# Attention entries on un-normalised input, and rotary partners fetched by DMA: a fused fp32 block on one core

## The reference: what is computed

```python
def apply_rope(x, cos, sin):            # DA and DSA; SWA rotates part of the head only
    x1, x2 = jnp.split(x.astype(jnp.float32), 2, axis=-1)
    return jnp.concatenate([x1 * c - x2 * s, x2 * c + x1 * s], axis=-1)
# SWA: softmax over a band with a sink, output times silu(gate)
h = h + diff_attention(rms_norm(h, da_norm), da_w_qkv, ...)   # a = p1 - lam * p2, 8 heads
h = h + dsa_attention(rms_norm(h, dsa_norm), dsa_w_in, ...)   # 16 heads, masked by the index
```

## Time and profile before

| | us |
|---|---|
| median of three runs | 2396.76 |
| lowest, highest | 2393.91, 2399.07 |
| profiled execution, its own time | 2399.34 |
| its span | 2397.2 |
| mean granted TensorE clock of it | 0.941 of full speed |

### The profile page before, as it was taken

The page is one execution under the profiler, slowest core; times in us unless marked ns, Lnnn a source line. Parts: engine busy times, 40 slices in busy tenths (PEclk is TensorE's granted clock), DMA queues, the critical chain, the costliest instruction groups (busy, mean ns, idle before and its releaser), DMA issues. The chain is left out here.

```text
span 2397.2 us, 41216 instructions
## 1 busy us (share of the span) xinstructions
PE 2217.2 (92%) x15151; PEld 1943.4 (81%) x15151; DVE 1466.3 (61%) x3053; ACT 1014.1 (42%) x1857; POOL 47.8 (2%) x37
## 2 busy tenths in 40 slices
PE   5999996979996799997999999989899889999998
PEld 3777775857774688885999999977777679999997
DVE  6778786354554566765566663359667656666522
ACT  4555554234443345554444342233455444443322
POOL 1000000000000000000000000021200000000000
PEclk7999996989997899997999999988999879999998
DMA  4533412343210211111233333311111123333330
GB/s 121 142 101 102 108 53 57 92 75 79 55 35 20 69 54 47 49 44 36 85 91 87 87 107 90 85 53 36 50 36 44 35 62 88 87 87 94 104 92 35
DMA packets 361349, 172.36 MB, mean 72 GB/s; under 512 B 67647, under 2 KB 359336, under 8 KB 361256
## 3 DMA queue, kind: packets, MB, share of 16 engines
q1 hardware_dynamic: 360616, 170.28, 26.0%
q0 software_dynamic: 640, 0.87, 0.3%
HBM read 168.68 MB, written 2.16 MB: 71 GB/s over the span
## 5 line engine op out<-in xcount | busy, mean ns | idle before, releaser
L277 PE MATMUL ps<-h_parts,parts 128*128 128x264 f32 (+1 forms) x8672 | 1337.7, 313 | 28.8 <-DVE h_parts L301 16.4
L277 PEld LDWEIGHTS ps<-h_parts,parts 128*128 128x128 f32 x8672 | 1196.8, 190 | 128.7 <-issue 32.6
L236 ACT ACTIVATE parts<-ring 128x1024 fp32r<-128x1024 f32 (+1 forms) x286 | 311.1, 1092 | 736.4 <-PE ps L277 501.6
L252 DVE TENSOR_TENSOR parts<-ring,parts 128x1024 fp32r<-128x1024 f32 (+1 forms) x270 | 341.4, 1268 | 248.1 <-ACT parts L236 247.1
L277 PE MATMUL ps<-wide_parts,parts 128*128 128x264 f32 (+1 forms) x1152 | 351.0, 305 | 0.0
L277 PE MATMUL ps<-up_hidden,parts 128*128 128x264 f32 x1408 | 257.8, 285 | 1.7 <-PEq L2209 1.7
L277 PEld LDWEIGHTS ps<-wide_parts,parts 128*128 128x128 f32 x1152 | 219.6, 191 | 9.0
L277 PEld LDWEIGHTS ps<-up_hidden,parts 128*128 128x128 f32 x1408 | 217.9, 188 | 2.1 <-issue 2.1
L2192 DVE TENSOR_TENSOR up_u<-ps,norm_rstd 128x264 f32<-128x264 f32 x176 | 75.3, 429 | 162.6 <-PE ps L277 155.2
L2462 DVE TENSOR_TENSOR res<-ps,res 128x264 f32<-128x264 f32 (+1 forms) x64 | 27.4, 432 | 102.4 <-PE ps L277 96.0
L277 PE MATMUL ps<-gated_high,parts 128*128 128x512 f32 x256 | 82.8, 404 | 3.4 <-DVE wide_parts L1124 3.4
(11 more groups left out here) (295 smaller groups left out, 2428.8 us busy)
## 6 DMA issues: line engine op xcount, KB each, us to landing
ring<-in_ffn_w_up SPq DMA_DIRECT2D x88, 512.0 KB, 3.8
ring<-in_ssm_w_in SPq DMA_DIRECT2D x48, 512.0 KB, 4.1
ring<-in_ffn_w_down SPq DMA_DIRECT2D x32, 704.0 KB, 4.5
ring<-in_att_w_in SPq DMA_DIRECT2D x48, 256.0 KB, 3.6
ring<-in_da_w_qkv SPq DMA_DIRECT2D x24, 512.0 KB, 3.7
ring<-in_dsa_w_in SPq DMA_DIRECT2D x24, 512.0 KB, 3.7
ssm_prefix<-prefix_rows SPq DMA_DIRECT2D x32, 256.0 KB, 4.1
ring<-in_ssm_w_out SPq DMA_DIRECT2D x16, 512.0 KB, 4.1
```

What stands on the lines that cost most here:

```text
L236: self.nc.scalar.activation(self.part(st, u, 0), self.slot(u, st.kt), ACT.Copy).then_inc(self.w_high, 1)
L252: self.nc.vector.tensor_tensor(self.part(st, u, 1), self.slot(u, st.kt), self.part(st, u, 0).bitcast(F32), ALU.subtract).then_inc(self.w_l ...
L277: m = self.nc.tensor.matmul(out, w[:, n], b, start=start and f == j == 0, stop=stop and f == st.kt - 1 and j == 2)
```

## The change

**Entry of SWA and DA.** A class `Residual` takes the place of `Norm` with `post`. After each residual add ACT writes gain * x (without the second rstd) as the high part and, after it, the square; DVE makes the low part. PE runs the first sums tile by tile while tiles arrive: SWA units 0, 1, 2 in banks 0, 1, 2 (9 matmuls a tile), in DA the four sums of q and k (12 matmuls a tile). The squares are added up by DVE (`dve_sum`), PE sums once over the partitions (`pe_sum`), ACT makes the second rstd (`act_rstd`). It is applied later: the cos and sin tables are multiplied by it (`tables`), v is scaled per token (`pe_tokens`, `act_tokens`, and `vtok` in four or five scaled copies), and DVE multiplies SWA's gate by it (`take_gate`) before Silu.

**Rotary in DA and DSA.** `rot` is gone. Behind the high part of the weights that follow q, and of those that follow k, ACT issues four DMAs (`turn`), each of 32 partitions x 528 fp32 (67.6 KB) from `raw` to `turned`, with the halves of a head swapped; the sine table now carries the sign. DVE waits for them, and t2 = turned * sin. Index rotary and SWA rotary stay products.

**Order in DA.** The v pieces of item s move from slots 4 and 5 of the pass ahead to slots 0 and 1 of its own attention pass; q and k of item s+1 stand in slots 2 to 5. DVE's low weight parts of DA move from behind the probabilities' normalisation to behind the maximum. In DSA PE's list loses its two `rot` calls and keeps the rest.

```diff
-            rot2[b + d + 32, m] = -1
+            rot2[b + d + 32, m] = 1
...
+    sin2 = np.where(d < 32, -1, 1).astype(np.float32)[:, None] * sin2
     return np.concatenate([eye, ones, tri, rot1, rot2, before, causal, cos2, sin2, inv1], axis=1)
...
+    def pe(self, pe, st, sums, done):
...
+        for f in range(KT):
...
+            for u, c, w, bank in sums:
+                m = k.product(st, u, k.ps[:, bank, 0:w], k.hx(c, w), tiles=[f])
+                if f == KT - 1:
+                    m.then_inc(done, 1)
...
+    def pe_sum(self, pe):
+        pe.wait_ge(self.k.nsem["accumulated"], self.base["accumulated"] + 1 + KT)
+        self.sum_over_partitions(self.T, 6, self.k.acc)
...
+        k = self.k
+        pe.wait_ge(k.nsem["rstd_steps"], self.base["rstd_steps"] + 4)
+        for t in range((self.T + P - 1) // P):
+            c, n = TILES[t]
+            m = k.nc.tensor.matmul(k.ps[0:n, 7, P + t:P + t + 1], k.rstd[:, c:c + n], k.ident[:, 0:1], start=True, stop=True)
+        m.then_inc(k.nsem["tokens"], 1)
...
+    def act(self, act):
...
+        for f in range(KT):
+            act.wait_ge(n["post_steps"], self.base["post_steps"] + 2 * f + 2)
+            k.nc.scalar.activation(self.spread.high(f), self.full(f), ACT.Copy, scale=k.col(self.gain + f)).then_inc(n["high"], 1)
+            k.nc.scalar.activation(self.squares(f), self.full(f), ACT.Square).then_inc(n["squared"], 1)
...
+    def act_rstd(self, act):
+        self.rms(act, 1, self.T, 6, 2)
...
+    def act_tokens(self, act, rtok):
+        k, n, at = self.k, self.k.nsem["tokens"], self.base["tokens"]
...
+        k.nc.scalar.activation(rtok[:, 0:4], k.ps[:, 7, P:P + 4], ACT.Copy).then_inc(n, 1)
...
+    def low(self, dve, f):
+        k, s = self.k, self.spread
+        dve.wait_ge(k.nsem["high"], s.base["high"] + f + 1)
+        k.nc.vector.scalar_tensor_tensor(s.low(f), self.full(f), k.col(self.gain + f), s.high(f).bitcast(F32),
+                                         ALU.mult, ALU.subtract).then_inc(k.nsem["low"], 1)
...
+    def dve(self, dve):
...
+        for f in range(KT):
...
+            nc.vector.scalar_tensor_tensor(self.tmp(f % 2), self.y(f), k.col(self.post_gain + f), k.rstd[:, 0:SEQ], ALU.mult, ALU.mult).then_inc(n["post_steps"], 1)
+            dve.wait_ge(n["post_steps"], at["post_steps"] + 2 * f + 1)
+            nc.vector.tensor_tensor(self.res(f), self.res(f), self.tmp(f % 2), ALU.add).then_inc(n["post_steps"], 1)
+            if f:
+                self.low(dve, f - 1)
+        self.low(dve, KT - 1)
...
+    def dve_sum(self, dve):
...
+        for f in range(KT):
+            dve.wait_ge(n["squared"], at["squared"] + f + 1)
+            k.nc.vector.tensor_tensor(k.acc[:, 0:self.T], k.acc[:, 0:self.T], self.squares(f), ALU.add).then_inc(n["accumulated"], 1)
...
+        dve.wait_ge(self.k.nsem["rstd_steps"], self.base["rstd_steps"] + 4)
+        v.tensor_tensor(cos, from_cos, self.k.rstd[:, 0:self.T], ALU.mult).then_inc(n, 1)
+        v.tensor_tensor(sin, from_sin, self.k.rstd[:, 0:self.T], ALU.mult).then_inc(n, 1)
...
-                    k.product(st, q, ps[:, q % 2, :], k.hx(0, SEQ), before=(lambda f: pre.ready(pe, f)) if first else None).then_inc(sem["lin_done"], 1)
+                    k.product(st, q, ps[:, q % 2, :], k.hx(0, SEQ)).then_inc(sem["lin_done"], 1)
...
-                            rot(s, 2), vtr(s)
+                            rot(s, 2)
+                            if isinstance(s, int) and s == 0:
+                                pre.pe_tokens(pe)
+                            vtr(s)
...
-                pre.pe(pe)
-                for q in range(4):
-                    piece(0, q)
+                pre.pe(pe, st, [(u, 0, SEQ, u) for u in range(3)], sem["lin_done"])
+                piece(0, 3)
+                pre.pe_sum(pe)
                 step(0)
...
-                        nc.scalar.activation(gate[:, bass.ds(2 * i + q - 4, 1), :].rearrange("p a t -> p (a t)"), src, ACT.Silu).then_inc(sem["lin_free"], 1)
+                        act.wait_ge(sem["lin_free"], 6 * i + q + 1)
+                        nc.scalar.activation(gate_tile(i, q - 4), gate_tile(i, q - 4), ACT.Silu).then_inc(sem["silu"], 1)
...
-                    nc.scalar.activation(vt[:], ps[:, 2, :].rearrange("p (t d) -> p t d", t=4)[:, :, 0:64], ACT.Copy).then_inc(sem["v"], 1)
+                    for t in range(4):
+                        m = nc.scalar.activation(vt[:, t, :], ps[:, 2, t * P:t * P + 64], ACT.Copy, scale=rtok[:, t:t + 1])
+                    m.then_inc(sem["v"], 1)
...
+                            if s == 0:
+                                pre.act_tokens(act, rtok)
                             vtok(s)
...
+                pre.act_rstd(act)
...
+                def take_gate(s, j):
+                    dve.wait_ge(sem["lin_done"], 6 * s + 5 + j)
+                    dve.wait_ge(sem["lin_free"], 6 * s + 4 + j)
+                    v.tensor_tensor(gate_tile(s, j), ps[:, j, :], k.rstd[:, 0:SEQ], ALU.mult).then_inc(sem["lin_free"], 1)
...
+                            take_gate(s, q - 1)
...
-                    k.low_on_vector(dve, st, st.after(0, u, st.depth))
+                k.low_on_vector(dve, st, (0, 3))
+                pre.dve_sum(dve)
+                k.low_on_vector(dve, st, (0, 4))
+                k.low_on_vector(dve, st, (0, 5))
+                pre.tables(dve, k.cos1[:], k.sin1[:], k.cos1[:], k.sin1[:])
+                k.low_on_vector(dve, st, (1, 0))
...
-        slots = [[(q, whole)] for q in range(6)] + [[]]
+        slots = [[(4 + q if q < 2 else q - 2, whole)] for q in range(6)] + [[]]
...
-                def rot(s, q):
-                    if q == 0:
-                        pe.wait_ge(sem["lin_free"], NP * s + NP)
-                        wait(pe, sem["masked"], 10 * s)
-                    elif not diff:
-                        wait(pe, sem["o"], 5 * s)
-                    for b in range(2):
-                        m = nc.tensor.matmul(ps[:, 4 - 2 * q + b, 0:HALF], k.rot2, raw[:, q, b * HALF:(b + 1) * HALF], start=True, stop=True)
-                    m.then_inc(sem["rot"], 1)
...
                 def vtr(s):
+                    pe.wait_ge(sem["lin_free"], NP * s + NP)
                     wait(pe, sem["o"], 5 * s)
...
-                        if lin:
+                        if diff and q < 2:
+                            if att:
+                                piece(s, 4 + q, whole)
+                        elif lin:
...
-                            if att:
-                                rot(s, 0), rot(s, 1)
+                            if att and not tail:
+                                pre.pe_sum(pe)
                             if tail:
                                 trans(s - 1, 4)
...
                             if tail:
-                                pv(s - 1, 3), trans(s - 1, 4)
-                            if att:
-                                rot(s, 0)
-                            if tail:
-                                pv(s - 1, 4)
-                            if att:
-                                rot(s, 1)
+                                pv(s - 1, 3), trans(s - 1, 4), pv(s - 1, 4)
...
+                            pre.pe_tokens(pe)
+                            pe.wait_ge(k.nsem["tokens"], k.ncount["tokens"])
...
+                if diff:
+                    pre.pe(pe, st, [(q // 2, q % 2 * HALF, HALF, q) for q in range(4)], sem["lin_done"])
+                else:
+                    step(0, att=False, tail=False)
...
+                def turn(i, u):
+                    act.wait_ge(sem["lin_free"], NP * i + 2 * u + 2)
+                    wait(act, sem["rope"], 2 * i - 1 + u if not isinstance(i, int) or i else 0)
+                    for r in range(0, P, 32):
+                        act.dma_start(turned[r ^ 32:(r ^ 32) + 32, u, :], raw[r:r + 32, u, :]).then_inc(s_turned[u], 16)
...
-                    nc.scalar.activation(vt[:, 0:4, :].rearrange("p t d -> p (t d)"), ps[:, 6, :], ACT.Copy)
-                    nc.scalar.activation(vt[0:META, 4, :], ps[0:META, 7, 0:P], ACT.Copy).then_inc(sem["v"], 1)
+                    for t in range(4):
+                        nc.scalar.activation(vt[:, t, :], ps[:, 6, t * P:(t + 1) * P], ACT.Copy, scale=rtok[:, t:t + 1])
+                    nc.scalar.activation(vt[0:META, 4, :], ps[0:META, 7, 0:P], ACT.Copy, scale=rtok[0:META, 4:5]).then_inc(sem["v"], 1)
...
                             if j % 2:
                                 k.high(act, st, st.after(i, j // 2, st.depth))
+                                if j < 4:
+                                    turn(i, j // 2)
...
-                        if lin:
+                        if diff and q == 0 and att and not tail:
+                            pre.act_rstd(act)
+                        if att if diff and q < 2 else lin:
...
+                                if not tail:
+                                    pre.act_tokens(act, rtok)
                                 vtok(s)
...
```

(33 more changed lines are left out.)

120 lines of the change are left out of this document (67 added, 53 removed).

## The result

The changed kernel took 2376.05 us (median of 4 runs, 2373.68 to 2381.34) against 2396.43 for the kernel before (median of 4, 2393.91 to 2399.07). The ratio is 0.992, 95% interval 0.9904 to 0.9935: 20 us faster, where 43 were forecast and 2374 was the end of the range.

A forecast was written before the change was run, and what follows sets the result against it. PE bounds the loops (busy 92% of the span), chains through DVE and ACT the entries and tails. 10.9 - 1.2 + 6 + 11.1 + 4.4 + 7.2 + 5.3 = 43.7 off 2396.8 gives 2353.1, said as 2353.5; range 2341 to 2374.

The forecast's parts named there:

- only 0.7 of it delays what is behind: DSA's loop: a turn's four issues take 1.5 us on ACT, overlap the 1.06 high part, and delay later work 0.7.
- 7.6 less 1.6: DA's entry: earlier first scores, less 1.6 us for PE's half speed after a gap; gain 6 (3 to 8).
- nothing, PE covers it: SWA's later groups: two DVE gate products of about 0.7 us each cost nothing; if uncovered, 1.4 a group.
- DA's loop: DA's items: permutations leave PE, six items times 1.95 us less small ACT slips; gain 11.1 (8 to 12).
- with PE at 99% each item gets 1.95 shorter, if DVE has its partners in time: DA's loop: removing the permutations' 1.95 us from PE shortens each 30.05 us item equally, with the copies' landing hidden.
- DSA's loop: DSA's items: 2.0 us less 0.7 and 0.1 gives 1.2 an item, six items; gain 7.2 (1 to 11).
- an issue has no row on ACT ... I take SP's: DSA's loop: ACT's issue priced by SP's 0.373 us rather than POOL's 0.504, making 1.5 a turn.
- Rival (a): ACT's issues and work don't overlap: DSA's loop gains nothing, DA's slips double; about 2363 us, chance 0.17.
- Rival (d): Issues on ACT are dear in both loops: gains used up at about 0.75 us each, about 2423 at 1.0; chance 0.04.
- (b): SWA and DA entries give half, 8.5 of 16.9 us, as the second rstd is only moved; about 2362, chance 0.10.
- (e): DA and DSA partners land late, DVE waits for DMA and PE's freed time idles; about 2391 us, chance 0.02.
- Tails: Last items: DA gains 4.4 us (2 to 5.5); DSA's tail 4.3, together with its entry 5.3 (2 to 6).

The follow-up runs named there:

- rot_both: The changed kernel with the permutation product in place of ACT's copies in DA and DSA, new entries and order kept: 2384.82 us, ratio 0.9946 to the kernel before.
- swa_both: The changed kernel with SWA's v copied once unscaled and its gate left without the rstd and DVE's products: 2371.45 us, one run.
- sp_turn: The changed kernel with the same copies issued by SP between its weight loads instead of by ACT: 2356.63 us, ratio 0.9828 to the kernel before.

## Why the prediction was wrong, point by point

The main step that failed is the price of the copies' issues on ACT: 0.373 us each and "only 0.7 of it delays what is behind", where the runs show 0.61 each and ACT idle for 1.7 to 1.8 a turn, with a loss of clock behind it for which the sum had no term. It turned DSA's gain into a loss.

*Entries.* Right in mechanism: -10.2 for -10.9 in SWA, -6.1 for -6 in DA. In DA's term "7.6 less 1.6" doesn't follow from the two times beside it (864.6 less 857.3 is 7.3, and the 1.6 is already in the second); by those times the scores should have come 35.8 us after the first residual step, and they came after 37.1. By the lists shown above eight pieces, not seven, stood before DA's first scores, so both pieces (6.3 us) did move behind them, as that comparison needs. No gain of the copies shows here: with the product back, *rot_both* took 36.1, and executions with the copies between 36.1 and 37.1.

*SWA's groups.* Forecast +1.2, measured +5.2 with the stage's end. I priced v's four copies (0.55 measured a group, within my 0.25 to 1.0) and called DVE's gate products covered, "nothing, PE covers it". The cover was the high weight part, and the last group has none: 0.87 more there. And I priced no clock: 1.6 in that group. The groups from swa_both show that nothing else of the change costs time in them. The 0.9 at the stage's end is mostly neither of the two: with both edits that stretch is 40.0 us, against 40.2 in the change and 39.3 before. Its cause stays open, and the stretch up to DA's first residual step is 0.9 shorter.

*DA's loop.* Forecast -11.1, measured -3.2, all of it in the last four of the six items (0.85 each). The step that failed is "with PE at 99% each item gets 1.95 shorter, if DVE has its partners in time". The partners were in time. But the product had also filled PE's list while DVE normalised the last tile. Without it PE reaches the transposition early and waits. Of the 1.95 (30.9 to 28.9) an item got 1.25 with SP's issues (29.65), 1.0 with ACT's (29.9). Placing the low weight part later gave 0.27 back; the last 0.4 are partly DVE's lateness at the first scores (0.19), and partly open.

*DSA's loop.* Forecast -7.2, measured +5.5: the largest miss, in the step "an issue has no row on ACT ... I take SP's". The gain of 2.0 without a stall was right: sp_turn's item is 24.8 against 26.7. The stall was mis-sized. An issue is 0.61, not 0.373, since SP's row was of another kind of transfer; SP needs 0.59 for these. POOL's 0.504, which I had as the other end, was nearer. 4 x 0.61 less 0.9 of cover left 1.5, with ACT's start 1.7 to 1.8, where I had 0.7. At full clock that cost an item 1.8 us where the sum had 0.8, and the gain was gone. Then the gaps drew the clock down, another 1 us or so in most items, for which the sum had no term at all. The size of the +5.5 is partly the profiled execution's clock; +2.0 is what four others show. Rival (a) had the place right (what stands behind the issues) and its 1.5 is near the 1.7 measured, but its mechanism was wrong, since the issues do overlap with the high part; that the numbers meet is luck. It had DSA gain nothing, and DSA lost. Rival (d) had the sign's mechanism and put its threshold at 0.75 us an issue over both loops; DSA alone lost at 0.61. Rivals (b) and (e) fell: the entries gave all of their term, and a landing was waited for once, 1.8 us.

*Tails.* In DA -4.6 for -4.4. Up to the last item's first scores the new order alone gives 3.7 (*rot_both*), ACT's copies 1.1 more. In DSA -3.3 for -4.3, but not by merit of the copies alone. The term rests on the earlier trace rows, where each permutation ran at half clock. *rot_both* has the same DSA lists as the kernel before, and its last item kept the clock. From DVE's t1 to the scores, in *rot_both* and in the change:

```profile
1880.79 1.31 DVE L2000 TENSOR_TENSOR wide<-wide,rcos 128x528 f32<-128x528 f32 x2
1886.72 0.80 PE L1738 MATMUL ps<-wide 64*128 64x128 f32 x4 [1.71 <-DVE wide L2009]
```

```profile
1886.48 1.31 DVE L1974 TENSOR_TENSOR wide<-wide,rcos 128x528 f32<-128x528 f32 x2
1890.90 0.80 PE L1723 MATMUL ps<-wide 64*128 64x128 f32 x4 [1.34 <-DVE wide L1979]
```

That is 8.7 us before, 5.9 in *rot_both*, 4.4 in the change. So the copies gain 4.3 over a half-clock execution, as I had it, and 1.5 over one that keeps its clock. Against this the issues make t1 start 2.0 us later in the item: the change's last item is 26.4, *rot_both*'s 25.9, *sp_turn*'s, without that stall, 24.4. That the tail's term nearly came out is luck of the clock.

## What to carry to other kernels

Before moving work off a busy engine, ask what it covered and what the replacement puts in whose list. A DMA issue is an instruction of the engine that issues it: price it by the same kind of transfer, let it stand under a long instruction or ahead of nothing that anyone waits for, or give it to an idle engine. And price the clock: in DSA 1.8 us of waiting an item cost about 1 more in clock, in SWA's last group 1.4 of waiting came with 1.6. One profiled execution is a thin base for a term that depends on the clock: the same DSA code gave +2.0 and +5.5.

## What the hardware showed that I had not expected

- The issue of a copy from SBUF to SBUF: 0.61 us on ACT for 32 or 16 partitions, 0.47 in DSA and 0.57 in DA for 64 (medians), 0.59 on SP for 32; the 512 KB weight loads take SP 0.37. Smaller copies were not cheaper to issue.
- In DSA landing hardly depended on size: 2.0 us for 33 and for 66 KB, 2.4 for 132 KB. In DA, issued by ACT, the medians were 2.0, 2.6 and 3.8.
- The same five items' matmuls took 127.6 us of PE at a mean clock of 0.92 and 118.1 at 1.00; the clock fell in items with gaps of 1.1, 0.4 and 0.4 us, and in four other executions of the same code the first two items kept 1.00. In SWA one stretch at the low level was worth 1.6 us a group, and came or stayed away at the same wait.
- The same DSA tail, with the permutation, took 59.8 us in one execution and 56.2 in another; each permutation there took 2.13 us in the first and 1.16 in the second.
